# Two scan directions on the four quadrants of TensorE: the backward direction's small products in exchanged partition halves, issued between the forward ones

## The reference

```python
def step(S, inp):
    rt, wt, kt, vt, at, bt = inp
    sa = jnp.einsum('bhvk,bhk->bhv', S, at)
    S = S * wt[:, :, None, :] + sa[..., None] * bt[:, :, None, :] + vt[..., None] * kt[:, :, None, :]
    return S, jnp.einsum('bhvk,bhk->bhv', S, rt)
```

## Time and profile before

| | |
|---|---|
| profiled execution | 2470.64 us, of which the span of the core's instructions is 2468.7 us |
| median of three runs | 2470.89 us |
| TensorE busy | 2196.2 us (89% of the span) |
| scan of layer 0, of layer 1 | 436.0 to 675.3 us, 1695.4 to 1921.7 us |
| granted clock of TensorE over the span | 0.954 of full speed |

### The profile page before, as it was taken

How to read it: one execution, slowest core, us unless ns; L and a number is a source line. 1 busy time by engine, 2 the same in 40 slices (tenths; PEclk the granted TensorE clock), 3 DMA queues, 4 the chain that set the end, 5 groups by cost and what they waited for, 6 DMA issues and landing times. The chain is left out here.

```text
span 2468.7 us, 58810 instructions
## 1 busy us (share of the span) xinstructions
PE 2196.2 (89%) x26490; PEld 1414.7 (57%) x26490; DVE 745.4 (30%) x1642; ACT 510.6 (21%) x1122; POOL 287.7 (12%) x461
## 2 busy tenths in 40 slices
PE   6989999899899999999999698998999899977774
PEld 2434443798844444446566464555898688744443
DVE  1023334766531011310100122456676311300002
ACT  2022322333230000301111132323332301200001
POOL 0000000433200000001111200002443000011111
PEclk9999999899999999999999889998999899998887
DMA  7139816000032222348999811110000344899993
GB/s 273 69 109 330 315 46 230 3 4 4 10 104 78 70 83 103 145 173 314 381 385 385 311 47 45 62 47 2 4 4 4 137 153 154 284 338 384 379 384 132
DMA packets 182934, 400.23 MB, mean 162 GB/s; under 512 B 6656, under 2 KB 29952, under 8 KB 182496
## 3 DMA queue, kind: packets, MB, share of 16 engines
q1 hardware_dynamic: 170528, 361.94, 40.8%
q0 software_dynamic: 8576, 23.08, 2.5%
q10 hardware_dynamic: 3648, 12.45, 1.7%
HBM read 365.47 MB, written 31.98 MB: 161 GB/s over the span
## 5 line engine op out<-in xcount | busy, mean ns | idle before, releaser
L472 PE MATMUL ps<-H,memory 128*128 128x512 f32 (+2 forms) x1728 | 618.3, 515 | 11.9 <-DMA memory<-in_w_in 10.1
L472 PEld LDWEIGHTS ps<-H,memory 128*128 128x128 f32 (+1 forms) x1728 | 330.1, 192 | 287.9 <-issue 251.3
L707 PE MATMUL ps<-memory 64*64 64x64 f32 (+1 forms) x12672 | 384.2, 223 | 40.5 <-issue 16.2
L707 PEld LDWEIGHTS ps<-memory 64*64 64x64 f32 x12672 | 364.9, 136 | 56.1 <-issue 34.4
L965 PE MATMUL ps<-memory 128*32 128x256 f32 x5120 | 306.6, 402 | 59.0 <-DMA memory<-in_eu 57.4
L472 PE MATMUL ps<-memory 128*128 128x512 f32 (+4 forms) x960 | 339.7, 504 | 17.1 <-DVE memory L1431 10.6
L965 PEld LDWEIGHTS ps<-memory 128*32 128x32 f32 x5120 | 193.2, 116 | 170.2 <-issue 91.2
L472 PEld LDWEIGHTS ps<-memory 128*128 128x128 f32 (+2 forms) x960 | 176.7, 186 | 170.4 <-issue 142.2
L1872 POOL TENSOR_TENSOR memory<-memory,cons 128x256 f32<-128x256 f32 x160 | 128.0, 813 | 192.3 <-DVE memory L1560 139.1
L990 PE MATMUL ps<-memory 128*32 128x256 f32 x2560 | 144.8, 380 | 4.9 <-ACT memory L1311 3.8
L1936 POOL DMA_DIRECT2D expert_rows<-memory x128 | 69.3, 541 | 437.0 <-DVE memory L1807 416.1
(11 more groups left out here) (251 smaller groups left out, 1792.8 us busy)
## 6 DMA issues: line engine op xcount, KB each, us to landing
memory<-in_eg SPq DMA_DIRECT2D x32, 2048.0 KB, 19.0
memory<-in_eu SPq DMA_DIRECT2D x32, 2048.0 KB, 24.9
memory<-in_ed SPq DMA_DIRECT2D x32, 2048.0 KB, 21.6
memory<-in_w_ada SPq DMA_DIRECT2D x24, 2048.0 KB, 10.3
memory<-in_w_in SPq DMA_DIRECT2D x20, 2048.0 KB, 9.1
expert_rows<-memory SPq DMA_DIRECT2D x4, 3456.0 KB, 23.7
memory<-in_w_out SPq DMA_DIRECT2D x4, 2048.0 KB, 8.5
memory<-expert_rows ACTq DMA_DIRECT2D x19, 384.0 KB, 7.0
```

The costliest lines, as they stand in the source:

```text
L472: ins = mm(ps[0:M, bank, 0:w], lhs(k), rhs(k), start=(k == 0), stop=(k == n - 1))
L707: ins = mm(out[cols, j], lhs[rows, j, :], rhs[rows, j], start=(n == 0), stop=(n == len(terms) - 1))
```

## The change

The products of the backward direction that were on the diagonal quadrants and came behind those of the forward direction are put on the other two quadrants and issued in turn with the forward ones: the turned keys (`turns`), the first gram with queries, the second one, the first two terms of `readout`, and `update`. For this U is left in exchanged halves (`solve` now has `held` = `made` = d), and the values of direction 1 are made twice, plain and exchanged (`Vt`, `Vx`: 8 products and one ScalarE copy more in each step). The wide gram of direction 1 becomes two narrow ones, the one without queries alone in `last_gram` after `solve` (8 products more in each step with outputs). The state's term of the backward readout goes to a bank of its own, so that `read(k, 1)` adds twice. Both readouts stand in level 1, both updates in level 3; `read` of both directions stands ahead of `totals` and `operands` in level 1. VectorE sums backward with one reversed scan in place of a scan and two operations, and masks the two backward grams with queries in one operation.

```diff
         inv = [piece(3) for d in range(2)]
-        raw = [piece(3) for d in range(2)]
+        raw = [piece(3), piece(1)]
+        VB = [piece(2) for p in range(2)]
...
-                 "Vt": [[quads(raw[d][:, 512 * p:512 * p + 256]) for d in range(2)] for p in range(2)],
+                 "Vt": [[quads(raw[0][:, 512 * p:512 * p + 256]), quads(VB[p][:, 0:256])] for p in range(2)],
+                 "Vx": [[quads(raw[0][:, 512 * p:512 * p + 256]), quads(VB[p][:, 256:512])] for p in range(2)],
...
+        GR = [[quads(piece(2), 2) for d in range(2)] for p in range(2)]
+        for n, name in enumerate(("Grb", "Grk")):
+            TWICE[name] = [[GR[p][d][:, n] for d in range(2)] for p in range(2)]
...
-        sums = quads(piece(1))
...
@@ -699,13 +701,15 @@
                 def heads(signal, *products):
 
                     for j in range(RJ):
-                        for n in range(len(products[0]) - 1):
+                        for n in range(max(len(terms) for out, *terms in products)):
                             for out, *terms in products:
+                                if n >= len(terms) or terms[n] is None:
+                                    continue
+                                used = [m for m in range(len(terms)) if terms[m]]
                                 lhs, rhs, held, made = terms[n]
                                 for h in range(2):
                                     rows, cols = (slice(CH * (h ^ x), CH * (h ^ x) + CH) for x in (held, made))
-                                    ins = mm(out[cols, j], lhs[rows, j, :], rhs[rows, j], start=(n == 0),
-                                             stop=(n == len(terms) - 1))
+                                    ins = mm(out[cols, j], lhs[rows, j, :], rhs[rows, j], start=(n == used[0]), stop=(n == used[-1]))
                                 if signal and j == RJ - 1 and n == len(terms) - 1:
                                     ins.then_inc(sem(signal), 1)
 
@@ -725,28 +729,41 @@
                     for d in both:
                         if k >= 2:
                             pe.wait_ge(sem("state"), states(l, k - 1, d))
+                            if streams(l, k - 2):
+                                pe.wait_ge(sem("read"), 2 * readouts(l, k - 2) - 1 + d)
                         if k:
                             pe.wait_ge(sem("masked"), nth(l * STEPS + k - 1, d))
-                        heads("values", (part(d, 0, 0), (V[:, :, columns(k, d)], eye, 0, 0)))
-
-                def grams(k, d):
+                    v = [V[:, :, columns(k, d)] for d in both]
+                    heads(None, (part(1, 0, 0), (v[1], eye, 0, 0)))
+                    heads("values", (part(0, 0, 0), (v[0], eye, 0, 0)), (part(1, 1, 0), (v[1], eye, 0, 1)))
+
+                def grams(k):
                     N, p = l * STEPS + k, k % 2
+                    for d in both:
+                        pe.wait_ge(sem("values_held"), nth(N, d))
+                        if k >= 2 and streams(l, k - 2):
+                            pe.wait_ge(sem("read"), 2 * readouts(l, k - 2) - 1 + d)
+                        if streams(l, k):
+                            pe.wait_ge(sem("queries"), 2 * readouts(l, k) - 1 + d)
                     wide = 2 if streams(l, k) else 1
-                    pe.wait_ge(sem("values_held"), nth(N, d))
-                    if k >= 2 and streams(l, k - 2):
-                        pe.wait_ge(sem("read"), 2 * readouts(l, k - 2) - 1 + d)
-                    if streams(l, k):
-                        pe.wait_ge(sem("queries"), 2 * readouts(l, k) - 1 + d)
-                        heads(None, (part(d, 0, 1), (ONCE["bE2"][d], TWICE["Rq"][p][d], 0, 0)))
-                    heads("grams", (ps[:, 4 * d + 1, 0:256 * wide].rearrange("p (x j n) -> p j x n", x=wide, n=CH),
-                                    (ONCE["bKk"][d], ER[p][d][:, 0:wide].rearrange("p x j n -> p j x n"), 0, 0)))
+                    left = (ps[:, 1, 0:256 * wide].rearrange("p (x j n) -> p j x n", x=wide, n=CH),
+                            (ONCE["bKk"][0], ER[p][0][:, 0:wide].rearrange("p x j n -> p j x n"), 0, 0))
+                    if not streams(l, k):
+                        heads("grams", left)
+                        return
+                    heads(None, (part(0, 0, 1), (ONCE["bE2"][0], TWICE["Rq"][p][0], 0, 0)),
+                          (part(1, 1, 0), (ONCE["bE2"][1], TWICE["Rq"][p][1], 0, 1)))
+                    heads("grams", left, (part(1, 1, 1), (ONCE["bKk"][1], TWICE["Rq"][p][1], 0, 1), None))
+
+                def last_gram(k):
+                    heads("grams", (part(1, 0, 1), (ONCE["bKk"][1], TWICE["E3"][k % 2][1], 0, 0)))
 
                 def turns(k):
                     for d in both:
                         if k:
                             pe.wait_ge(sem("u_copied"), nth(l * STEPS + k - 1, d))
-                        heads(None, (part(d, 3, 0), (ONCE["bE2"][d], eye, 0, 0)))
-                        heads("turns", (part(d, 3, 1), (ONCE["bKk"][d], eye, 0, 0)))
+                    heads(None, *((part(d, 3, 0), (ONCE["bE2"][d], eye, 0, d)) for d in both))
+                    heads("turns", *((part(d, 3, 1), (ONCE["bKk"][d], eye, 0, d)) for d in both))
 
                 def correct(k):
                     N, p = l * STEPS + k, k % 2
@@ -762,22 +779,28 @@
                     for d in both:
                         pe.wait_ge(sem("rhs_copied"), nth(N, d))
                         pe.wait_ge(sem("inverse"), inverses(N, 5, d))
-                    heads("u", *((part(d, 3, 1), (TWICE["XT"][p][d], ONCE["RHS"][d], d, 0)) for d in both))
-
-                def readout(k, d):
+                    heads("u", *((part(d, 3, 1), (TWICE["XT"][p][d], ONCE["RHS"][d], d, d)) for d in both))
+
+                def readout(k):
                     N, p = l * STEPS + k, k % 2
-                    pe.wait_ge(sem("u_copied"), nth(N, d))
-                    if k + 1 < STEPS:
+                    for d in both:
+                        pe.wait_ge(sem("u_copied"), nth(N, d))
+                        if k + 1 < STEPS:
+                            pe.wait_ge(sem("masked"), nth(N + 1, d))
+                    own = [((ONCE["U"][d], TWICE["Grb"][p][d], d, 0), (TWICE["Vx"][p][d], TWICE["Grk"][p][d], d, 0)) for d in both]
+                    past = [(ONCE["S"][d], TWICE["Rq"][p][d], 0, 0) for d in both]
+                    heads("readout", (part(0, 1, 0), *own[0], past[0]), (part(1, 1, 0), *own[1], None),
+                          (part(1, 0, 0), None, None, past[1]))
+
+                def update(k):
+                    N, p = l * STEPS + k, k % 2
+                    for d in both:
+                        pe.wait_ge(sem("u_copied"), nth(N, d))
                         pe.wait_ge(sem("masked"), nth(N + 1, d))
-                    heads("readout", (part(d, 1, 0), (ONCE["S"][d], TWICE["Rq"][p][d], 0, 0),
-                                      (ONCE["U"][d], TWICE["Grb"][p][d], 0, 0), (TWICE["Vt"][p][d], TWICE["Grk"][p][d], 0, 0)))
-
-                def update(k, d):
-                    N, p = l * STEPS + k, k % 2
-                    pe.wait_ge(sem("u_copied"), nth(N, d))
-                    pe.wait_ge(sem("masked"), nth(N + 1, d))
-                    heads("step", (part(d, 0, 0), (TWICE["Bt"][p][d], ONCE["U"][d], 0, 0),
-                                   (TWICE["Kt"][p][d], TWICE["Vt"][p][d], 0, 0)))
+                        if streams(l, k):
+                            pe.wait_ge(sem("read"), 2 * readouts(l, k) - 1 + d)
+                    heads("step", *((part(d, 0, 0), (TWICE["Bt"][p][d], ONCE["U"][d], d, 0),
+                                     (TWICE["Kt"][p][d], TWICE["Vx"][p][d], d, 0)) for d in both))
 
                 def join(k, n, d):
                     N = l * STEPS + k
...
                         solve(k - 1)
-                    grams(k, 1)
+                    last_gram(k)
                     if more:
                         turns(k)
                     for n in range(len(LEVELS)):
...
-                            readout(k - 1, n)
-                        if k and 2 <= n < 4:
-                            update(k - 1, n - 2)
+                        if k and n == 1 and streams(l, k - 1):
+                            readout(k - 1)
+                        if k and n == 3:
+                            update(k - 1)
                         join(k, n, 1)
                         grow(k, n, 0)
...
                 solve(STEPS - 1)
-                for d in both:
-                    readout(STEPS - 1, d)
+                readout(STEPS - 1)
...
                         act.wait_ge(sem("values"), nth(l * STEPS + k, d))
-                        act.copy(flat(TWICE["Vt"][k % 2][d]), part(d, 0, 0)).then_inc(sem("values_held"), 1)
+                        if d == 0:
+                            act.copy(flat(TWICE["Vt"][k % 2][0]), part(0, 0, 0)).then_inc(sem("values_held"), 1)
+                        else:
```

(47 more changed lines are left out.)

1 line of the change is left out of this document (removed).

## The result

After the change the kernel takes 2498.69 us (median of 4 runs, 2495.41 to 2502.06), against 2470.75 before (2470.18 to 2472.47). The ratio is 1.0114, 95% interval 1.0098 to 1.0130: 28 us more. The forecast was 2483, 12 more, with a range up to 2495, so the direction was right and the size less than half of it. The profiled execution took 2499.55 us at a span of 2497.8.

A forecast was written before the change was run, and what follows sets the result against it. Bound: TensorE, with VectorE and ScalarE in the levels' loop and pauses for instruction packets. Full steps +11, layer 1's steps 1 to 4 +1.6, steps 0 -1.6, scan ends +1.5: +12.5 on 2470.64, so 2483 us (2476 to 2490; wide range 2461 to 2495).

The forecast's parts named there:

- Level 1, "both: 4.87": Level 1 of a full step, given both readouts: 4.87 us for 4.35.
- ten full steps: Steps 1 to 7 of layer 0 and 5 to 7 of layer 1: +1.1 us each, +11 together.
- Level 2, "5.03": Level 2 of a full step: loses its update, but reads delay VectorE's add by 1.35, so 5.03 us for 4.25.
- Level 3, "3.95": Level 3 of a full step, with both updates on four quadrants: 3.95 us for 3.89.
- Level 0, "3.42": Level 0 of a full step, without its readout: 3.42 us for 4.36.
- the start, "+0.1": Full step before its levels: cheaper grams and turns against dearer solve and two bare waits, taken as +0.1 us.
- The pauses, "+0.5 to +2.4, I take +1.1": Full step's growth in us: +0.55 from parts plus pauses for instruction packets, up to +1.9 from new ones.
- The rule set beside it: Skill's rule that crossing instruction blocks is mostly hidden: no pause term, only the pause-free parts' sum, about +7 us.
- (a): Rival: pauses go into the new waits at turns, level 0 and level 2; 2456 us, chance 0.12.
- (b): Rival: the products' own price in turns, updates, readouts, grams and solve reaches the end; -37, 2434 us, chance 0.06.
- (c): Rival: VectorE's operands take 0.42 us each, levels -0.6, pauses stay; 2470 us, no change, chance 0.20 with small losses.
- (d): Rival: the new bursts pay in full, +2.4 us a step; 2496 us, chance 0.16.

The follow-up runs named there:

- both apart: Changed kernel with readout and its reads in level 0, turns and updates each one direction after the other: 2471.16 us, 0.9996 of the kernel before.
- the shifted kernel: Changed kernel with 128 empty TensorE instructions around `values(0)` of layer 0, moving later packet boundaries by half a packet: 1.0112 of the kernel before.
- the burst: Kernel before with 224 more products on four quadrants at couple in step 4 of layer 0: that step 42.2 us, whole time 2483.31 (one run).
- version 2: Changed kernel with readout and VectorE's reads both moved to level 0: 2477.22 us, 1.0029 of the kernel before.

## Why the forecast was right in direction and wrong in size

By the ratios, the 28 us are 8 for the readout's place, 13 for the reads' place, 8 for turns and updates on four quadrants, and what is left, -1 (0.9996), for exchanged halves, grams, values and all. By the intervals each of the first three is uncertain by 4 to 6 us, and moved boundaries can be in each.

**Level 1, "both: 4.87".** This is the first step that failed. The work was priced rightly: with readout and levels on full supply it takes 4.85 (step 4 of both apart, level 0). The wait was missed. The forecast looked for everyone who waits for turns, for solve and for operands, but not for who waits for the moved readout: ScalarE's `decays`, whose place in its queue didn't move. Level 1 took 1.2 us more than forecast in step 4 and 1.3 in the mean. Step 7 bears this out in part: it has readout, reads and updates but no `decays` of a next step and no operands. TensorE waits for no copy in its level 1 there, and its two instances together are 0.3 us shorter than before. But its level 1 still takes 5.5 us in layer 0 and 6.5 in layer 1, with pauses of 0.47 and 1.44, so the burst of both readouts is dear without ScalarE's wait too. The forecast counted step 7 among ten full steps at +1.1 each.

**Level 2, "5.03".** The mechanism was right, the reads stand ahead of operands, and so was the statement that their short durations wouldn't save it: operands again took 0.95. It measured 5.30, 0.27 more: the three reads end at 587.05 and operands' long ones begin at 587.64, with totals and the first operand between. For the reads alone the forecast had +1.35 (the +0.8 is what is left of it once the update is gone), 11 us in the eight steps that have operands. Moving them took level 2 from 5.40 to 3.69, 1.7 a step or 14 us in eight, as much as the 13 of the ratios. So the term was mis-sized by 3 us of the 28.

**Level 3, "3.95".** Right where the clock is full (3.91, 4.02). Nothing in the forecast spoke of the clock, since before it never fell in a scan. The falls put 1.5 us into three of six levels, 0.75 a step in the mean, a term that the forecast had at nothing. Whether it adds to the sum stays open: the shifted kernel has two falls fewer and the same sum.

**Level 0, "3.42", and the start, "+0.1".** Level 0 measured 3.17 in step 4 and 3.28 in the mean. The start grew by 1.0. Its own parts came about as forecast: turns 2.03 with the bare copy for 1.86, the last gram with the wait behind it 0.93 for 0.97. What grew are pauses, 1.11 in correct and 1.07 in solve of step 4, where before one of 0.97 stood.

**The pauses, "+0.5 to +2.4, I take +1.1".** Right in kind and mis-sized, by less than the waits. The idle time put down to issue grew by 33 us in both of PE's queues taken together, but by 9.6 on TensorE's products (27.2 to 36.8); the forecast held 5.5 (1.1 less the 0.55 of longer parts, ten times). Taking apart the two densest bursts makes the kernel 8 us faster, though their own price of 1.9 a step comes on top: waits for the turned copy and for VectorE's adds cover it. The sum let no packet be shorter than 3.7 us; the burst showed 3.5 to 4.0.

**The rule set beside it** (the Trainium skill, Runtime: NRT & Kernel Launch, Instruction fetch mechanics: crossing a block mostly hidden) does not hold for this stream: the trace shows up to 1.92 us unhidden per block of 64 four-quadrant products. On two quadrants, where 512 records follow each other without a pause, the trace agrees with it.

**Together.** The forecast lacks 16 of the 28 us. By the traces level 1 is some 10 of them (1.3 in eight steps), level 2 3 and the pauses 4; these are rough and overlap, for level 1 holds pauses too.

**The rivals.** (a) The pauses don't go into the new waits: they grew (27.2 to 36.8) beside waits of 0.86, 1.00 and 1.81 in step 4. (b) The products' own price doesn't reach the end: taking more than half of it back (turns and updates) did not make the kernel slower but 8 us faster. (c) failed with operands at 0.95. (d), 2496, was nearest in number, but by another way: it put +2.4 a step on the bursts, and apart they give back 0.8.

**Still open.** How much of the 8 us of turns and updates is fewer pauses, how much the clock and how much the place of the boundaries: either alone gave nothing that can be measured. Why one gram less made more pauses; and whether the reads in level 0 are worth the same in a kernel with an even instruction stream.

## What to carry to other kernels

When an instruction is moved, list all who wait for its signal, on every engine, and for each ask where it stands in its own queue: the waiter that stays behind holds up everything behind it. Before halving the price of small products, check the rate at which their instructions come: here a packet of 256 lasts no less than 3.5 to 4.0 us, so what counts is the number of instructions and how evenly they lie. And an engine's late operation is best moved to a level in which that engine idles: that paid 13 us in one kernel and, with a shorter sum of decays, 5 in the other.

## What was not expected of the hardware

224 products of 64x64x64 take 13.7 us, on two quadrants and on four alike. The granted clock fell in four steps of the scans, 0.69 over a level of 5.59 us, although in the 30 us before each fall TensorE had never stood longer than 1.8 us at a stretch in two of them, 2.5 in the third and 1.0 in the fourth. And 8 products fewer a step made the scans of version 2 6.0 us longer, with more pauses and no fall of the clock.
